# Modulation vectors formed as columns, and the first layer's weight sums moved into its up-projection

## What is computed

```python
m_lat = split(silu(c) @ w_mod[i] + b_mod[i], 6)          # six vectors of 1024: shift, scale, gate, shift, scale, gate
h_lat = rmsnorm(x_lat, g_pre_mix[i]) * (1 + m_lat[1]) + m_lat[0]
m_ctx = split(silu(c_ctx) @ w_mod[i] + b_mod[i], 6)      # layer 0 only: the same weights with c_ctx
h_ctx = rmsnorm(x_ctx, g_pre_mix[i]) * (1 + m_ctx[1]) + m_ctx[0]
y_lat = mixer(h_lat, h_ctx)
x_lat = x_lat + m_lat[2] * rmsnorm(y_lat, g_post_mix[i])
h = rmsnorm(x_lat, g_pre_ffn[i]) * (1 + m_lat[4]) + m_lat[3]
u = depthwise_conv(h @ w_up, w_dw) + b_dw                # 1024 -> 2 * 2816
gate, val = split(u, 2)
x_lat = x_lat + m_lat[5] * rmsnorm((silu(gate) * val) @ w_down, g_post_ffn[i])
```

## Time and profile before

| | us |
|---|---|
| median of 3 executions | 2483.79 (2473.08 to 2486.47) |
| profiled execution | 2476.99 |
| its span | 2474.6 |
| TensorE busy | 2414.3 |
| VectorE busy | 1844.6 |
| ScalarE busy | 1209.1 |
| POOL busy | 612.5 |
| mean granted clock | 0.987 |

### The profile page before, as it was taken

How to read it: one execution, slowest core, us unless ns; L and a number is a source line. 1 busy time by engine, 2 the same in 40 slices (tenths; PEclk the granted TensorE clock), 3 DMA queues, 4 the chain that set the end, 5 groups by cost and what they waited for, 6 DMA issues and landing times.

```text
span 2474.6 us, 32113 instructions
## 1 busy us (share of the span) xinstructions
PE 2414.3 (98%) x11124; PEld 1955.1 (79%) x11124; DVE 1844.6 (75%) x2786; ACT 1209.1 (49%) x1948; POOL 612.5 (25%) x473
## 2 busy tenths in 40 slices
PE   7989999999899999999999999999999999999998
PEld 3878888888788788888888787766887888888886
DVE  5467676767637988888655879998579888887556
ACT  3356565666643544544454542244645544445542
POOL 0058586874033300010000321100432001010002
PEclk9999998999999999999999999999999999999999
DMA  6046465652432455555865567711314555558655
GB/s 271 27 145 175 124 174 160 187 144 68 136 124 78 120 146 140 141 132 139 247 221 187 179 196 183 157 39 47 115 56 128 146 144 132 134 139 265 211 183 178
DMA packets 153203, 366.31 MB, mean 148 GB/s; under 512 B 14432, under 2 KB 15712, under 8 KB 153056
## 3 DMA queue, kind: packets, MB, share of 16 engines
q1 hardware_dynamic: 107056, 242.69, 28.4%
q0 software_dynamic: 44416, 116.93, 21.9%
q10 hardware_dynamic: 1584, 4.85, 0.6%
HBM read 303.07 MB, written 136.31 MB: 178 GB/s over the span
## 4 chain that ended last, share of the span: by engine, by line
PE 71%; DVE 18%; POOL 4%; DMA 3%; issue 3%; ACT 1%; SPq 0%; DVEq 0%; POOLq 0%; ACTq 0%
PE psum L2305 21%; PE psum L2307 21%; PE psum L2306 21%; DVE acts L2215 3%; DVE acts L2217 3%; PE psum L2521 2%; DMA set<-mod_w 1%; POOL set L837 1%; DVE weights_f32r L1850 1%; PE psum L2510 1%; PE psum L2511 1%; POOL set L836 1%; DVE acts L2219 1%; DMA low<-x_t 1%; POOL low L837 1%
## 5 line engine op out<-in xcount | busy, mean ns | idle before, releaser
L2305 PE MATMUL psum<-acts_f32r,weights_f32r 128*128 128x512 f32 x1536 | 606.4, 395 | 9.3 <-DVE acts_f32r L1610 3.0
L2307 PE MATMUL psum<-acts_f32r,weights_f32r 128*128 128x512 f32 x1536 | 599.1, 390 | 0.0
L2306 PE MATMUL psum<-acts_f32r,weights_f32r 128*128 128x512 f32 x1536 | 598.6, 390 | 0.0
L955 ACT ACTIVATE weights_f32r<-low 128x512 fp32r<-128x512 f32 (+2 forms) x471 | 303.8, 660 | 449.0 <-DVE low L1996 257.4
L2305 PEld LDWEIGHTS psum<-acts_f32r,weights_f32r 128*128 128x128 f32 x1536 | 288.9, 188 | 71.8 <-issue 6.2
L2307 PEld LDWEIGHTS psum<-acts_f32r,weights_f32r 128*128 128x128 f32 x1536 | 288.7, 188 | 61.3
L2306 PEld LDWEIGHTS psum<-acts_f32r,weights_f32r 128*128 128x128 f32 x1536 | 289.1, 188 | 58.7 <-issue 0.5
L862 POOL TENSOR_TENSOR low<-low 128x512 f32<-128x512 f32 x91 | 133.8, 1471 | 691.9 <-ACT low L1194 685.9
L2305 PE MATMUL psum<-high_f32r,weights_f32r 128*128 128x512 f32 (+1 forms) x485 | 192.1, 396 | 0.0
L2307 PE MATMUL psum<-high_f32r,weights_f32r 128*128 128x512 f32 (+1 forms) x485 | 186.9, 385 | 0.0
L2306 PE MATMUL psum<-high_f32r,weights_f32r 128*128 128x512 f32 (+1 forms) x485 | 186.8, 385 | 0.0
(11 more groups left out here) (254 smaller groups left out, 4702.0 us busy)
## 6 DMA issues: line engine op xcount, KB each, us to landing
low<-units SPq DMA_DIRECT2D x130, 512.0 KB, 4.2
set<-mod_w POOLq DMA_DIRECT2D x80, 512.0 KB, 3.9
low<-gated_sums SPq DMA_DIRECT2D x110, 256.0 KB, 4.5
low<-weight_sums SPq DMA_DIRECT2D x88, 256.0 KB, 4.1
gated_sums<-low SPq DMA_DIRECT2D x22, 768.0 KB, 3.5
low<-units SPq DMA_DIRECT2D x66, 256.0 KB, 5.0
weight_sums<-units POOLq DMA_DIRECT2D x14, 1024.0 KB, 10.1
residual<-low SPq DMA_DIRECT2D x48, 256.0 KB, 2.0
```

The costliest lines, as they stand in the source:

```text
L955: return act.activation(out, in_, ACT.Copy, scale=scale)
L2305: pe.matmul(out, wl, xh, start=first, stop=False, skip_group_check=continued)
L2306: pe.matmul(out, wh, xl, start=False, stop=False, skip_group_check=continued)
L2307: return pe.matmul(out, wh, xh, start=False, stop=last, skip_group_check=continued)
```

## The change

It has two parts.

**Start-up.** `mod_vectors` forms scale and shift as columns at once: for each block k, eight products whose stationary operand is a 128x128 block of the weights and whose moving operand is the two columns of `C_SC`. The row copies, the transposes and their semaphores go. The squares of x are no longer added by VectorE: they rotate through three buffers, and TensorE sums each with eight products of one column, accumulating over k. All of this stands before the shift vector, the spread behind shift's second block, and eight spins behind it. VectorE takes up shift after six of its eight scalings.

**Weight sums.** Layer 0 gets the groups of layer 1 (12 parts), and they are issued in the first twelve steps of its up-projection loop, one behind each gated sum. The counts on `summed` come from a list of the order, `sums_order`.

```diff
-W_GROUPS = (tuple((m, min(m + 2, KB)) for m in range(0, KB, 2)), tuple((m, min(m + 4, KB)) for m in range(0, KB, 4)))
...
+W_GROUPS = tuple((m, min(m + 4, KB)) for m in range(0, KB, 4))
...
+        order += [("weights", 1, n) for n in range(4 * len(W_GROUPS))] * layer
+        for p in range(FB):
+            order += [("first", layer, p)] if p < KB else [("second", layer, p - KB)]
+            order += [("weights", 0, p)] * (layer == 0 and p < 4 * len(W_GROUPS))
+            order += [("third", layer, p - KB)] * (p >= KB)
...
-            return f(F_ACC) if n in (0, CB) else f((F_SQ if n < CB else F_LATSQ) + (n + 1) % 2 * L)
+            return f(F_SQ + n % 3 * L) if n < CB else f(F_ACC) if n == CB else f(F_LATSQ + (n + 1) % 2 * L)
...
-                    if (t * CB + k) % 3 == 2 and t * CB + k < 72:
-                        weight_sum(0, (t * CB + k) // 3)
...
                     else:
                         second_sum(layer, p - KB)
+                    if layer == 0 and p < 4 * len(W_GROUPS):
+                        weight_sum(0, p)
...
                 square_full(k, A(k))
-                if k == 3:
-                    act.wait_ge(rows_done, 1)
-                    copy(ROWS[0:2, 0:HALF], PS[0:2, 0:HALF]).then_inc(row_out, 1)
             std(N_A, D, CB, 1)
-            act.wait_ge(rows_done, 2)
-            act.wait_ge(cols_out, 1)
-            copy(ROWS[0:2, 0:HALF], PS[0:2, 0:HALF]).then_inc(row_out, 1)
             act.wait_ge(shift_out, 1)
...
-            for k in range(1, CB):
-                add_square(k)
...
+            dve.wait_ge(cols_out, 1)
+            mod_columns(1, N_SCALE, 6)
...
-            for k in range(CB):
+            for k in range(CB - 2):
                 scaled(x_block, col(C_AV), RT, k)
-            dve.wait_ge(rows_done, 2)
-            dve.tensor_copy(ROWS[0:2, HALF:L], PS[0:2, HALF:L]).then_inc(row_out, 1)
             dve.wait_ge(mod_mm, 1)
-            mod_columns(0, N_SHIFT)
+            mod_columns(0, N_SHIFT, 2)
...
+            def mod_vectors(w, at, k, b):
+
+                for c in range(CB):
+                    mm = pe.matmul(bank(b, 2, at + 2 * c), w[:, c * P:(c + 1) * P], S[:, C_SC + 2 * k:C_SC + 2 * k + 2],
+                                   start=k == 0 and c == 0, stop=k == CB - 1 and c == CB - 1)
+                return mm
+
             spin(16, 5)
             for k in range(CB):
-
                 pe.wait_ge(scale_in[k // 2], 16)
-                for half in range(2):
-                    mm = pe.matmul(PS[0:2, half * HALF:(half + 1) * HALF], S[:, C_SC + 2 * k:C_SC + 2 * k + 2],
-                                   scale_w(k)[:, half * HALF:(half + 1) * HALF], start=k == 0, stop=k == CB - 1)
-            mm.then_inc(rows_done, 1)
-            pe.wait_ge(row_out, 2)
-            for c in range(CB):
-                mm = pe.transpose(bank(6, 2, N_SCALE + 2 * c), ROWS[0:2, c * P:(c + 1) * P], ident[0:2, 0:2])
+                mm = mod_vectors(scale_w(k), N_SCALE, k, 6)
             mm.then_inc(cols_out, 1)
-            spin(14, 5)
+            spin(16, 5)
             for k in range(CB):
-                if k == 2:
-                    pe.wait_ge(sq_used, CB - 1)
-                    col_sums(F_ACC, N_A, True, True).then_inc(sums_out, 1)
-
+                pe.wait_ge(sq_ready, k + 1)
+                for c in range(CB):
+                    mm = pe.matmul(bank(7, 1, N_A + c), sq(k)[:, c * P:(c + 1) * P], ones[:, 0:1],
+                                   start=k == 0 and c == 0, stop=k == CB - 1 and c == CB - 1)
+                mm.then_inc(sums_out if k == CB - 1 else sq_used, 1)
+            for k in range(CB):
                 pe.wait_ge(shift_in[k], 16)
...
+                mm = mod_vectors(shift_w(k), N_SHIFT, k, 2)
+                if k == 1:
                     spread(src=F_ACC)
...
             mm.then_inc(mod_mm, 1)
+            spin(8, 0)
```

More of the change, by code:

```diff
@@ L130, in op_done, with sums_order @@
     return M_FFN[layer] + 12 + 7 * p + i + 1
-W_GROUPS = (tuple((m, min(m + 2, KB)) for m in range(0, KB, 2)), tuple((m, min(m + 4, KB)) for m in range(0, KB, 4)))
-def weights_summed(layer, n):
-    return 16 * (layer * (6 * len(W_GROUPS[0]) + 3 * KB) + 6 * (n // 4) + (0, 2, 4, 5)[n % 4])
-def gated_summed(layer, n):
-    return weights_summed(layer, 4 * len(W_GROUPS[layer])) + 16 * n
+W_GROUPS = tuple((m, min(m + 4, KB)) for m in range(0, KB, 4))
+def sums_order():
+    order = []
+    for layer in range(2):
+        order += [("weights", 1, n) for n in range(4 * len(W_GROUPS))] * layer
[3 more added lines that the diff above has]
+            order += [("third", layer, p - KB)] * (p >= KB)
+    issued, done, count = {}, {}, 0
+    for kind, layer, n in order:
+        issued[kind, layer, n] = 16 * count
+        count += 2 if kind == "weights" and n % 4 < 2 else 1
+        done[kind, layer, n] = 16 * count
+    return issued, done
+SUMMED_BEFORE, SUMMED = sums_order()
 def dn_at(layer, t):
@@ L331, in build @@
         sums_out, std_ready, diag_ready, rt_out = sem("sums_out"), sem("std_ready"), sem("diag_ready"), sem("rt_out")
-        rows_done, row_out, cols_out = sem("rows_done"), sem("row_out"), sem("cols_out")
+        cols_out = sem("cols_out")
         ctx_sq, ctx_added, kv_sq, shift_out, h_used, kr_turned, kr_folded = (
@@ L418, in build @@
         CQ, CKV, KRT = [f(F_A + k * L) for k in range(3)], f(3072, KEYS), f(4352, KEYS)
-        ROWS = f(F_RT)
         def tap_diag(i, t):
@@ L669, in load_down @@
                     if j == 0:
-                        sp.wait_ge(summed, weights_summed(layer, 4 * len(W_GROUPS[layer])))
+                        sp.wait_ge(summed, SUMMED["weights", layer, 4 * len(W_GROUPS) - 1])
                     src = s_d[layer][w_n, j]
@@ L684, in load_down @@
                     elif g_n == 1:
-                        sp.wait_ge(summed, gated_summed(layer, j + 1))
+                        sp.wait_ge(summed, SUMMED["first", layer, j])
                     else:
-                        sp.wait_ge(summed, gated_summed(layer, KB + 2 * j + (2 if g_n == 4 else 1)))
+                        sp.wait_ge(summed, SUMMED["third" if g_n == 4 else "second", layer, j])
                     src = t_d[layer][j, g_n]
@@ L804, in weight_sum @@
                 group, part = divmod(n, 4)
-                m0, m1 = W_GROUPS[layer][group]
+                m0, m1 = W_GROUPS[group]
                 rows = (m1 - m0) * P
@@ L809, in weight_sum @@
                 sums = s_d[layer][:, m0:m1].rearrange("i m p n -> (m p) i n")
-                wait(pool, summed, weights_summed(layer, n))
+                pool.wait_ge(summed, SUMMED_BEFORE["weights", layer, n])
                 if part == 0:
@@ L891, in first_sum @@
                 pool.wait_ge(n_out, 16 * (FB * layer + j + 1))
-                pool.wait_ge(summed, gated_summed(layer, j))
+                wait(pool, summed, SUMMED_BEFORE["first", layer, j])
                 pool.dma_start(sums[:, 1:3], sums[:, 3].unsqueeze(1).to_broadcast([P, 2, HALF]),
@@ L898, in second_sum @@
                 pool.wait_ge(g_out, 16 * (FB * layer + KB + j + 1))
-                pool.wait_ge(summed, gated_summed(layer, KB + 2 * j))
+                pool.wait_ge(summed, SUMMED_BEFORE["second", layer, j])
                 pool.dma_start(t_d[layer][j, 2:4].rearrange("i p n -> p i n"), g_d[layer][j][:, HALF:L].unsqueeze(1).to_broadcast([P, 2, HALF]),
@@ L905, in third_sum @@
                 pool.wait_ge(n_out, 16 * (FB * layer + KB + j + 1))
-                pool.wait_ge(summed, gated_summed(layer, KB + 2 * j + 1))
+                pool.wait_ge(summed, SUMMED_BEFORE["third", layer, j])
                 pool.dma_start(t_d[layer][j, 4], t_d[layer][j, 2], accum_op=ADD, max_dma_last_dim=4 * HALF).then_inc(summed, 16)
@@ L939, in _ @@
             down(1)
-            for n in range(4 * len(W_GROUPS[1])):
+            for n in range(4 * len(W_GROUPS)):
                 weight_sum(1, n)
@@ L1576, in add_square @@
             def add_square(n):
-                first = n in (1, CB + 1)
                 dve.wait_ge(sq_ready, n + 1)
-                if not first:
-                    dve.wait_ge(sq_used, n - 1 if n < CB else n - 2)
+                if n > CB + 1:
+                    dve.wait_ge(sq_used, n - 2)
                 dve.tensor_tensor(f(F_ACC), f(F_ACC), sq(n), ADD).then_inc(sq_used, 1)
```

25 lines of the change are left out of this document (7 added, 18 removed).

## The result

| | before | after |
|---|---|---|
| median, us | 2478.43 (2470.2 to 2486.47) | 2512.86 (2507.42 to 2514.87) |
| ratio, 95% interval | | 1.0136 [1.0092, 1.0179] |
| span of the profiled execution, us | 2474.6 | 2512.8 |
| mean granted clock | 0.987 | 0.974 |

The change makes the kernel 1.4% slower. The forecast was 2506 with a range of 2488 to 2526 and 0.85 for slower: the time lies in the range, 7 us above the forecast. The terms under it did less well than their sum, and most of what follows is on that.

The account below looks back on a forecast made before the run. TensorE, busy 98% of the span, was taken as the bound, through its instructions, waits and clock. 2477.0 + 30.9 (start-up) - 5.4 (attention) + 0 (up-projection) = 2502.5, given as 2506 from the known times' middle; range 2488 to 2526.

Parts of the forecast that it names:

- The start-up: Before the first real product: three slow weight-load streams move it from 57.3 to 88.2, +30.9 us, bounds +25 and +38.
- the clock-weighted mark: First real product's start plus time lost by cold products behind it: 55.34 plus 2.0, counted as 57.3 us before.
- I take 0.11 and 0.19: Start-up streams: assumed us per record at full and lower clock, giving 21.8 us for a stream of 128 records.
- I let the clock rise once more: At the dense spread in shift: the clock recovers, so 31 of the last 96 records run full, 3.4 us.
- no rise at all: Start-up's upper bound, +38: no clock recovery at the spread, 0.196 us a record and cold products behind.
- the eight spins behind it should bring the products in at full clock: End of the start-up: spins behind the shift stream warm the first real products, so nothing is added.
- The attention: Weight sums leaving POOL's modulation loop remove a 2.0 us wait and 3.4 us of low clock: -5.4, bounds -10 and +2.
- the lows of vectors 4 and up: In the attention: low clock of 17.1 us behind the POOL wait shrinks to 10.2 without it, saving 3.4 us.
- the term of 0: Layer 0's up-projection: moved sums cost nothing, since POOL catches up and weight loads land; bounds 0 and +5.
- The clock that stays at 2.4 GHz: Rival in the start-up streams: full clock throughout, first product at 61.1, total 2475.4 or 2479; chance 0.10.
- Sums that come too late: Rival: POOL falls behind in the up-projection and the down-projection's third pass waits; +15, 2521; chance 0.10.
- An attention that gives nothing: Rival: POOL is held by something else, so the attention gives nothing back; 2511; chance 0.08.

Follow-up runs that it names:

- the start-up alone: Only the start-up part of the change on the kernel before, layer 0's weight sums staying in POOL's modulation loop: 2517.93 us, ratio 1.0159.
- the kernel with VectorE's squares: The changed kernel with VectorE adding the squares again and TensorE reducing the one sum by 8 products: 2485.27 us, ratio 1.0033 to the kernel before.
- the kernel with spins between: The changed kernel with 8 spins behind every 8 column products, replacing the 16 between streams: 2504.60 us, ratio 1.0122 to the kernel before.
- the sums alone: Only the move of layer 0's weight sums into the up-projection, start-up as in the kernel before: 2469.61 us, ratio 0.9976.

## Why the prediction came out as it did

**The start-up: the cause was right, the size was not.** The forecast's mark was 88.2, measured 100.9, and with four products at low clock behind it 101.7 by the clock-weighted mark. That makes +44.4 in place of +30.9, above the bound of +38. In the start-up alone, the same program in another execution, the mark is 91.5 and the term +34.2 (91.5 less 57.3; its first products are not cold), inside the bound. Term by term, in us:

| step | predicted | changed kernel | start-up alone |
|---|---|---|---|
| start of the scale stream | 10.3 | 11.2 | 10.5 |
| scale stream | 21.8 | 24.6 | 22.1 |
| 16 spins | 5.7 | 6.3 | 5.5 |
| squares | 21.8 | 24.7 | 22.4 |
| 32 records of shift | 6.1 | 6.8 | 6.8 |
| spread | 3.7 | 3.6 | 3.4 |
| 96 records of shift | 15.8 | 20.3 | 17.4 |
| last vector to first product | 3.0 | 3.4 | 3.3 |

The chief mistake is in "I take 0.11 and 0.19". The eight records of the earlier trace rows took 1.50 us in the chain, and I divided by eight. A chain piece of eight starts has seven spacings between them, 1.50 / 7 = 0.214, and 0.212 is what came out. The same goes for 0.79 / 7 = 0.113 at full clock, where I had taken 0.11, and so only the slow records came out too cheap. At 0.213 the 291 records that I priced as slow cost 6.7 us more, half of the miss of 13.5, and the two full streams come to 24.1 us each (3.4 + 97 x 0.213). Measured are 24.6 and 24.7, and in the start-up alone 22.1 and 22.4, because the 3.4 us at full clock were 2.9, 2.7, 5.5 and 5.2. It was a slip of reading and not of the chip: 0.19 is not twice 0.11, and in the measured streams the pace is 0.107 and 0.212.

The second mistake is "I let the clock rise once more", worth 3.2 us. It did not rise in the spread of the changed kernel (0.50 at 73 and at 80); it did in the start-up alone, where the same four records took 3.4 us and the stream behind was 3.0 us shorter. In the kernel with VectorE's squares it did not. So the assumption comes true in one of three executions. The upper bound did hold the case without it, "no rise at all", but at 0.196 a record: with its 322 slow records at 0.213 that bound is 5.5 us higher, +43.5, and the measured +44.4 is all but inside.

Third, "the eight spins behind it should bring the products in at full clock". At low clock they take 3.4 us, about what the path through VectorE and ScalarE takes that they were to cover (3.3 us in the kernel with spins between, where TensorE waits behind them), and the clock rose only at 102.8. So the products came in cold, and hardly late: 0.8 and 0.4 us.

**The attention: more came back than I gave it.** Predicted -5.4 with bounds of -10 and +2, measured -11.9 by the same clock-weighted mark (559.8 against 547.9). The named wait of 2.0 us went, and none took its place. At full speed the stretch is 5.0 us shorter, and TensorE's waits answer for it: 2.0 for POOL, 2.4 less for ScalarE (6.7 to 4.3), 0.8 less for weights from VectorE (1.7 to 0.9 in this stretch). I had priced only the first, though ScalarE's is the larger wait. That it is the sums' leaving which shortens it the other kernels bear out: ScalarE's wait is 11.3 us in the start-up alone, where the sums stayed, and 4.3 to 5.8 in the seven without sums in POOL's loop. The other 6.9 are fewer slices at low clock. I had counted 3.4 for the lows of vectors 4 and up that a wait made longer. What the nine executions say on it: with sums in the loop 19.3 and 17.1 us are lost to the clock, without them 0 to 11.5. The direction seems clear, but the last seven scatter by 11.5 among kernels that are alike there, and no experiment set the clock by itself in this stretch. That the sums' leaving is what shortens the lows is argued, not shown.

**The up-projection: the term of 0 left out a queue.** I looked at whether POOL would keep up and whether the weight loads would land; both were right. POOL caught up: the last weight sum landed at 1122.1, and SP issued the first load of one at 1279.6. I did not ask what the transfers of the parts, up to two of 2 MB, do to the store that SP issues while they are in flight, and whose buffer ScalarE must have back. It cost TensorE 3.9 us and 1.5 of clock in the changed kernel, and 2.7 with the sums alone; without the sums the wait is gone. Whether the store is held by the queues' order or by the share of the DMA engines no run separates. The whole stretch came out +2.7, inside the bounds of 0 and +5. By the rests of the table it is 1 to 4 us.

**The rest** of the span, 3.0 us (0.7 ahead of the feed-forward's norm and 2.3 in layer 1), is in code that the change doesn't touch. In layer 1 it is one wait of TensorE for VectorE:

```profile
PE psum L2302 <- DVE acts_f32r L2004: 2.6, 1, 2.6
```

In layer 1 of the other eight kernels the same wait is 0 to 1.3 us. No run looked for its cause; the two kernels nearest to the changed one have 981.3 and 982.3 us in that stretch against 984.3, and before 982.0, so it does not come with the change each time.

**The sum.** The errors are +13.5, -6.5 and +5.7: 12.7 us over the predicted difference of 25.5, which is the 38.2 of the spans. That the forecast missed by 7 only is luck in three pieces: the second error offsets half of the first; the medians differ by 34.4 where the profiled spans differ by 38.2, since the profiled execution is the slowest of the changed kernel's four; and the forecast started from a time before of 2480.4 where the median is 2478.4. 12.7 - 3.8 - 2.0 is the 6.9.

**The rivals.** The clock that stays at 2.4 GHz is refuted by the slices. Its price was close, though: 61.1 to the first product, and the rest of the changed kernel's start-up is 59.2. Sums that come too late did not appear. An attention that gives nothing is refuted by the wait for POOL, which is gone in every kernel without sums in POOL's loop, and by the 5.0 us at full speed; how much more of the 11.9 comes with the change is open.

## What to carry to other kernels

Many products of one or two columns are a poor trade for a few wide ones even where the engine never stands still: first ask at what clock such a stream runs, price it at the lower one, and leave the sums to an engine that is free. Spins between hold the clock but cost what they save; here even the clock's part taken off, the start-up stayed 5.1 us longer. A pace is a time between starts, so n records hold n - 1 of them; where a form's pace at the two levels of the clock does not come out a factor of two apart, as 0.107 and 0.212 do here, look at the reading again. When large transfers are moved, look at every small store on another queue whose buffer someone waits to reuse, not only at the engine that issues them. Where the clock falls at another place each time, one profile doesn't price a stage: the same start-up took 91.5 and 100.9 us.

## What the chip showed that was not expected

A stream of fp32 products whose only load is weights (PEld busy 1.00, two columns streaming) fell to 1.2 GHz 2.9 us after it began and stayed there for 27 us, until 5.6 us into the spins that followed. In five such streams of three executions the fall came 2.7 to 5.5 us after the start. With spins of 128 columns between groups of eight it held 2.4 GHz for 90 us. Two products of 512 columns (four records, 3.4 to 3.6 us at the lower clock) raised it in one of three executions.

A store of 768 KB that lands in 3.7 us in the median took 15.1 us when it was issued 2.4 us behind two transfers of 2 MB from HBM to HBM on another queue; these landed 12.7 and 20.7 us after their issue. Three more such stores, issued with a smaller HBM-to-HBM transfer in flight, landed within 1.0 us of it, after 8.8 to 9.9 us. Without these transfers the eleven stores took 3.5 to 4.7 us.
